# Reordering the end of the recurrent layer, with ScalarE squaring the residual of its last token tile

## The reference

```
x1 = x + (h * silu(gate)) @ w_out            # h: RG-LRU scan
kv = rmsnorm(x1, norm_kv) @ w_kv ;  k, v = split(kv)
k  = rmsnorm_per_head(k, k_norm)
u  = rmsnorm(x1, norm_b) @ w_in_b            # queries and gates of layer B
```

## Time and profile before

| what | us |
|---|---|
| median of 3 runs (1495.4, 1495.9, 1502.24) | 1495.9 |
| the profiled execution | 1499.04 |
| its span, first to last instruction | 1497.3 |
| PE busy | 1459.7 (97%) |
| DVE / ACT / POOL busy | 1035.9 / 700.1 / 259.3 |
| mean granted TensorE clock | 0.994 |

### The profile page before, as it was taken

The page is one execution under the profiler, slowest core; times in us unless marked ns, Lnnn a source line. Parts: engine busy times, 40 slices in busy tenths (PEclk is TensorE's granted clock), DMA queues, the critical chain, the costliest instruction groups (busy, mean ns, idle before and its releaser), DMA issues.

```text
span 1497.3 us, 31229 instructions
## 1 busy us (share of the span) xinstructions
PE 1459.7 (97%) x10634; PEld 1400.7 (94%) x10634; DVE 1035.9 (69%) x2235; ACT 700.1 (47%) x1577; POOL 259.3 (17%) x203
## 2 busy tenths in 40 slices
PE   7999999999999999999899999999998999999999
PEld 7999999999999999998899999999986788888888
DVE  6987857665688888887884534435277877777771
ACT  5433423427787777773362423414145544444440
POOL 0011111001334434443170000000011111111110
PEclk9999999999999999999999999999999999999999
DMA  6565655659855545555523222122345444443312
GB/s 239 168 206 215 214 179 196 219 191 328 301 185 154 170 150 169 169 169 166 176 90 105 76 75 92 51 99 69 94 140 178 122 131 131 124 110 103 106 51 78
DMA packets 215218, 224.20 MB, mean 150 GB/s; under 512 B 61488, under 2 KB 201776, under 8 KB 215088
## 3 DMA queue, kind: packets, MB, share of 16 engines
q1 hardware_dynamic: 202960, 213.19, 45.6%
q10 hardware_dynamic: 12128, 9.39, 1.9%
HBM read 136.33 MB, written 86.44 MB: 149 GB/s over the span
## 4 chain that ended last, share of the span: by engine, by line
PE 63%; DVE 5%; ACT 2%; DMA 1%; issue 1%; SPq 0%; POOL 0%; DVEq 0%; ACTq 0%
PE s_banks L790 22%; PE bank L1812 11%; PE bank L1464 11%; PE s_banks L1431 5%; PE s_banks L1762 3%; PE bank L1447 3%; PE bank L1794 2%; PE bank L1777 2%; PE bank L790 2%; PE bank L1798 2%; ACT m_p L1988 1%; DVE m_nmax L1865 1%; PE bank L1780 1%; DMA x_dram<-r_x 1%; DMA r_x<-xT_dram 1%
## 5 line engine op out<-in xcount | busy, mean ns | idle before, releaser
L1988 ACT ACTIVATE m_p<-s_banks,m_nm 128x192 f32<-128x192 f32 (+2 forms) x264 | 106.1, 414 | 193.0 <-DVE m_nm L1869 193.0
L1812 PE MATMUL bank<-m_y_hi,w_hi_a 128*128 128x256 f32 (+1 forms) x512 | 148.9, 291 | 2.8 <-DVE w_lo_a L910 1.9
L1812 PE MATMUL bank<-m_y_lo,w_hi_a 128*128 128x256 f32 (+1 forms) x512 | 143.8, 281 | 0.0
L1812 PE MATMUL bank<-m_y_hi,w_lo_a 128*128 128x256 f32 (+1 forms) x512 | 143.7, 281 | 0.0
L790 PE MATMUL bank<-a_hi,w_hi_a 128*128 128x352 f32 x384 | 123.6, 322 | 1.3 <-DVE a_out L690 1.1
L790 PE MATMUL bank<-a_hi,w_lo_a 128*128 128x352 f32 x384 | 123.9, 323 | 0.0
L790 PE MATMUL bank<-a_lo,w_hi_a 128*128 128x352 f32 x384 | 123.9, 323 | 0.0
L790 PE MATMUL s_banks<-b_hi,w_hi_b 128*128 128x352 f32 x336 | 111.2, 331 | 0.0
L1464 PE MATMUL bank<-r_y_hi,w_hi_a 128*128 128x264 f32 x384 | 109.3, 285 | 0.6 <-ACT r_std L1359 0.6
L1464 PE MATMUL bank<-r_y_lo,w_hi_a 128*128 128x264 f32 x384 | 109.1, 284 | 0.0
L1464 PE MATMUL bank<-r_y_hi,w_lo_a 128*128 128x264 f32 x384 | 108.8, 283 | 0.0
(11 more groups left out here) (216 smaller groups left out, 4605.3 us busy)
## 6 DMA issues: line engine op xcount, KB each, us to landing
w_raw_b<-weights_dram SPq DMA_DIRECT2D x26, 512.0 KB, 4.3
w_raw_a<-weights_dram SPq DMA_DIRECT2D x25, 512.0 KB, 4.4
sga_dram<-a_out SPq DMA_DIRECT2D x48, 176.0 KB, 3.0
r_xc_hi<-xc_hi_dram SPq DMA_DIRECT2D x32, 264.0 KB, 3.0
r_xc_lo<-xc_lo_dram SPq DMA_DIRECT2D x32, 264.0 KB, 3.1
r_xc<-xc_dram SPq DMA_DIRECT2D x32, 264.0 KB, 3.8
r_sg<-sga_dram SPq DMA_DIRECT2D x32, 264.0 KB, 3.5
r_x<-xT_dram SPq DMA_DIRECT2D x64, 132.0 KB, 2.1
```

Source lines behind the costliest of these rows:

```text
L1812: mm = nc.tensor.matmul(out_bank(ts, blk)[:, 0:width], w[pw][:, kt * P:(kt + 1) * P], (m.y_hi, m.y_lo)[px][tp][:, kt, 0:width], start=(n = ...
L1988: nc.scalar.activation(m.p[:, q, k, v0:192], s_banks[:, 2 * q + e, bp * 192 + v0:(bp + 1) * 192], ACT.Exp, bias=m.nm[:, q, k:k + 1], accum ...
```

## The change

Seven edits. (1) SP: of the four unit loads of turn (8,0), two are issued after the first block's store and the next x load, two after the second's (`gates_free`). (2) The token sum of tile 6 goes to bank 2 and its key sum to bank 3, which the gates no longer use; `out` of the last tile's blocks 1 and 3 then does not wait for the roots. (3) The last tile's key sum goes to bank 7 and runs after layer B's third block, not its first. (4) VectorE squares the last k after B's first block and normalises it after B's fourth (`key_square`, `key_norm`); ScalarE takes the root after B's third (`key_root`). (5) SP loads units 14 and 15 inside B's first pass, at its slots 4 and 5. (6) SP stores the last k and v at slot 6, not 4. (7) The squares of the last tile's residual (eight blocks) are made by ScalarE, in the turn of the block, ahead of that turn's high parts.

```
+        def last_tile(t):
+            return isinstance(t, int) and t == RN - 1
+        def last_sums(t):
+            return isinstance(t, int) and t == RN - 2
+        def key_bank(t):
+            return 5 if not isinstance(t, int) or t < RN - 2 else 3 if t == RN - 2 else 7
...
+            def gates_free(s, g, first):
+                if isinstance(s, int) and (s, g) == (RN, 0):
+                    for k in (first, first + 1):
+                        load_unit(eng, U_B1 + k, r.gates_done, 4 * NG * RN)
...
-                    if isinstance(s, int) and (s, g) == (RN, 0):
-                        for k in range(1, 1 + UNITS_GATE):
-                            load_unit(eng, U_B1 + k, r.gates_done, 4 * NG * RN)
                     if pair:
                         store_x1(pair, 0)
                         load_next(pair, 0)
...
                     if behind:
                         load_x(behind, 0)
+                    gates_free(s, g, 1)
                     if pair:
                         store_x1(pair, 1)
                         load_next(pair, 1)
                     if behind:
                         load_x(behind, 1)
+                    gates_free(s, g, 3)
...
-            for u in range(U_OUT_B - 2, U_OUT_B):
-                load_unit(eng, u, r.kv_mm, NB * RN)
...
+                if not last_tile(t):
+                    need(eng, r.sq_added, mth - 1)
+                    nc.vector.tensor_tensor(r.sq[:, q, :], r.x1[:, q, :], r.x1[:, q, :], ALU.mult).then_inc(r.sq_done, 1)
...
-                if known(s, 2, RN + 1) and g == 3:
-                    tail_norm(s - 2)
+                if known(s, 2, RN) and g == 3:
+                    key_norm(eng, s - 2)
...
                 if known(s, 0, RN - 1):
                     gates(s, g)
+                pair = back_pair(s, g)
+                for q in range(2) if pair and last_tile(pair[0]) else ():
+                    mth = NB * pair[0] + pair[1] + q
+                    eng.wait_ge(r.resid_done, mth + 1)
+                    need(eng, r.sq_added, mth - 1)
+                    nc.scalar.activation(r.sq[:, q, :], r.x1[:, q, :], ACT.Square).then_inc(r.sq_done, 1)
                 for unit in recurrent_units(s, g):
                     high_part(eng, unit)
...
-            if not last:
+            if last:
+                eng.wait_ge(r.kv_read, 2 * RN)
+            elif last_sums(t):
+                eng.wait_ge(r.gates_read, 4 * NG * RN)
+            else:
                 eng.wait_ge(r.resid_done, NB * (t + 1) + 2)
-            nc.tensor.matmul(bank[5][:, 0:RT], head_ones[:, :], r.k2[:, :], start=True, stop=True)\
+            nc.tensor.matmul(bank[key_bank(t)][:, 0:RT], head_ones[:, :], r.k2[:, :], start=True, stop=True)\
...
-                if blk == 1:
+                if blk == 1 and not last_sums(t - 1):
                     need(eng, r.std_done, t)
-                if blk == 3:
+                if blk == 3 and not last_sums(t - 1):
                     need(eng, r.kstd_done, t)
...
-            project_sync(eng, b1, {(1, 4): lambda: store_memory(eng, RN - 1), (1, 12): store_states, (PN, 0): start,
+            project_sync(eng, b1, {(1, 4): lambda: load_unit(eng, U_OUT_B - 2, r.kv_mm, NB * RN),
+                                   (1, 5): lambda: load_unit(eng, U_OUT_B - 1, r.kv_mm, NB * RN),
+                                   (1, 6): lambda: store_memory(eng, RN - 1), (1, 12): store_states, (PN, 0): start,
...
-                if isinstance(s, int) and (s, j) == (1, 0):
+                if isinstance(s, int) and (s, j) == (1, 2):
                     key_sum(eng, RN - 1, True)
...
+                if isinstance(s, int) and (s, j) == (1, 0):
+                    key_square(eng, RN - 1)
+                if isinstance(s, int) and (s, j) == (1, 3):
+                    key_norm(eng, RN - 1)
...
+                if isinstance(s, int) and (s, j) == (1, 2):
+                    key_root(eng, RN - 1)
```

More of the change, by code:

```diff
@@ L1166, in recurrent_sync, with key_square, key_norm @@
             run_steps(eng, 2, RN - 2, RN + 2, body)
-            for u in range(U_OUT_B - 2, U_OUT_B):
-                load_unit(eng, u, r.kv_mm, NB * RN)
             for i in range(2):
                 eng.wait_ge(r.x1_stored[i], 16 * RN * NB // 2)
+        def key_square(eng, t):
+            eng.wait_ge(r.kv_read, 2 * t + 1)
+            need(eng, r.kms_done, t)
+            nc.vector.tensor_tensor(r.k2[:, :], r.k[:, :], r.k[:, :], ALU.mult).then_inc(r.k2_done, 1)
+        def key_norm(eng, t):
+            eng.wait_ge(r.kstd_done, t + 1)
+            nc.vector.reciprocal(r.std[:, :], r.std[:, :]).then_inc(r.krec_done, 1)
+            eng.wait_ge(r.krec_done, t + 1)
+            nc.vector.scalar_tensor_tensor(out=r.k[:, :], in0=r.k[:, :], scalar=vec[:, KN, 0:1], in1=r.std[:, :],
+                                           op0=ALU.mult, op1=ALU.mult).then_inc(r.k_done, 1)
         def recurrent_vector(eng):
@@ L1228, in residual @@
                   .then_inc(r.x1_high, 1)
-                need(eng, r.sq_added, mth - 1)
-                nc.vector.tensor_tensor(r.sq[:, q, :], r.x1[:, q, :], r.x1[:, q, :], ALU.mult).then_inc(r.sq_done, 1)
+                if not last_tile(t):
+                    need(eng, r.sq_added, mth - 1)
+                    nc.vector.tensor_tensor(r.sq[:, q, :], r.x1[:, q, :], r.x1[:, q, :], ALU.mult).then_inc(r.sq_done, 1)
                 eng.wait_ge(r.x1_high, mth + 1)
@@ L1257, in tail_read @@
                 nc.vector.tensor_tensor(r.v[:, :], bank[7][:, 0:RT], r.rstd[:, :], ALU.mult).then_inc(r.kv_read, 1)
[L1258 to L1267, removed]
+                if not (isinstance(t, int) and t == RN - 1):
+                    key_square(eng, t)
             def turn(s, par, g):
@@ L1313, in recurrent_vector, with key_root @@
             eng.wait_ge(r.x1_free, 1)
+        def key_root(eng, t):
+            eng.wait_ge(r.rstd_done, t + 1)
+            eng.wait_ge(r.kms_done, t + 1)
+            nc.scalar.activation(r.std[:, :], bank[key_bank(t)][:, 0:RT], ACT.Sqrt, scale=1.0 / HEAD,
+                                 bias=eps[:, 0:1]).then_inc(r.kstd_done, 1)
         def recurrent_scalar(eng):
@@ L1353, in turn @@
                     need(eng, r.k_done, t)
-                    nc.scalar.activation(r.std[:, :], bank[5][:, 0:RT], ACT.Sqrt, scale=1.0 / D,
+                    nc.scalar.activation(r.std[:, :], bank[2 if last_sums(t) else 5][:, 0:RT], ACT.Sqrt, scale=1.0 / D,
                                          bias=eps[:, 0:1]).then_inc(r.std_done, 1)
[L1356 to L1360, removed]
+                if known(s, 2, RN) and g == 3:
+                    key_root(eng, t)
                 if known(s, 0, RN - 1):
                     gates(s, g)
+                pair = back_pair(s, g)
[4 more added lines that the diff above has]
+                    nc.scalar.activation(r.sq[:, q, :], r.x1[:, q, :], ACT.Square).then_inc(r.sq_done, 1)
                 for unit in recurrent_units(s, g):
@@ L1470, in token_sum @@
                 eng.wait_ge(r.resid_done, NB * (t + 1))
-                nc.tensor.matmul(bank[5][:, 0:RT], ones[:, :], r.acc[:, :], start=True, stop=True)\
+                if last_sums(t):
+                    eng.wait_ge(r.gates_read, 4 * NG * RN)
+                nc.tensor.matmul(bank[2 if last_sums(t) else 5][:, 0:RT], ones[:, :], r.acc[:, :], start=True, stop=True)\
                   .then_inc(r.ms_done, 1)
```

## The result

The change made the kernel **slower**: 1508.25 us (median of 6 runs, 1506.33 to 1510.24) against 1497.5 us (6 runs), a ratio of 1.0072 with a 95% interval of 1.0058 to 1.0085. The forecast was 1490.8 us, the range ended at 1496.0, and "slower by over 0.5%" had a chance of 0.04.

A forecast was written before the change was run, and what follows sets the result against it. PE, busy 97% of the span, was taken as the bound, with about 13 us to win in the seam. 2.6 + 2.7 - 0.9 + 0.9 - 0.8 - 0.3 + 0.9 = 5.1 us saved gave 1490.8 us, range 1487.5 to 1496.0.

The forecast's parts named there:

- Edits 3 and 4: Layer B's start: PE's 0.9 us for the square of k goes; VectorE's reciprocal without the key norm ahead gives nothing.
- The late key sum: Slower rival, chance 0.06: in layer B GpSimd waits for the later key sum; 2.4 us late takes back all 5.1.
- the 2.42 for a square beside GpSimd: Chain to the late key sum: evacuation and square take 1 us, or 3 with GpSimd in the way (2.42 against 0.43).
- Edit 1: Seam: earlier x of (6,6) gives 2.6 us at `out` of (7,0), 2.7 more by the clock; `kv` lead falls to 4.4.
- The two stores behind two unit loads each: SP's queue, (6,5) and (6,6): the latter's store lands after 1.74 us and 2.0 to 2.9 more.
- the 2.7 us of low clock: `out` of (7,0): the clock stays at 2.4 GHz, so it takes 2.93 us instead of 5.61; 2.7 won.
- Nothing in the seam explains that: Profiled execution 3.1 us above the median: not due to the seam, so the same saving was taken from the median.
- the latest start of tile 6's reciprocal: VectorE, behind `residual` of (7,0): the reciprocal starts between 702.0 and 703.3 us; 702.8 was taken.
- Edit 2: `out` of (7,1) and (7,3) no longer wait for the roots; 0.9 us won at (7,3), wait and slower restart.
- Edit 7: ScalarE's order delays VectorE: a new wait of 0.6 us (0.8 with restart) at `kv` of (7,4), 0.3 more at (7,6).
- no table was loaded at a square: ScalarE's squares: no table loads counted; rival with one load in each of four turns loses 5.1 us, chance 0.02.
- The last wait: `kv` of (7,7): the wait stays at 3.1 us, and the lower clock behind it at 1.7.

The follow-up runs named there:

- e13: e10 with the key norm back behind layer B's fourth block, and the store of k and first turn of old values back too: 1503.09 us, ratio 1.0044.
- e5: Edits 3 to 6 alone on the kernel before, with its banks, load order and VectorE's squares: 1507.73 us, ratio 1.0063.
- e6: Changed kernel with the key norm behind layer B's ninth block, not its fourth; store of k and first old values move along: 1507.29 us, ratio 1.0054.
- e7: Changed kernel with both moves: norm behind layer B's ninth block, GpSimd's wait for the key sum behind its unit 8: 1501.0 us, ratio 1.0018.
- e10: e7 without edit 7, and the square of k back at its old place ahead of VectorE's wait for `x1_free`: 1497.3 us, ratio 1.0008.
- e12: The kernel before, unchanged, measured and profiled once more: 1496.5 us, ratio 1.0001.
- e8: The kernel before with SP issuing the next x load ahead of the next unit load in each recurrent turn: 1500.2 us, ratio 1.0018.
- e1: Edits 1 and 2 alone on the kernel before: 1496.17 us, ratio 0.9997.
- e3: Changed kernel with edits 3 to 6 undone, so edits 1, 2 and 7 remain: 1500.81 us, ratio 1.0030.
- e11: e10 with edit 7 added (ScalarE squares the last tile): 1499.63 us, ratio 1.0023.
- e2: Changed kernel without edit 7 (VectorE squares the last tile's residual again): 1507.63 us, ratio 1.0078.
- e4: Changed kernel with GpSimd waiting for the key sum after its low part of unit 8, not unit 3: 1506.14 us, ratio 1.0056.

## Why the prediction was wrong

**Edits 3 and 4, the step that failed.** "VectorE takes up layer B's reciprocal ... without the key norm ahead of it; PE did not wait for it, so nothing." The norm was not saved but moved, and I looked for who waits for the reciprocal, not for who waits at the new place. There it stands in front of the square sums for the head sum, and the term that I had put at nothing measured 8.3 us of PE's time. The idle time of the trace that I had would not have shown it: behind the norm's new place VectorE idled 0.90 us in one block and 0.96 in each of three (of the 4.3 in the groups above, 0.48 lie ahead of that place), its last square sum ended at 776.84 + 0.51 = 777.35 us and PE reached the head sum at 777.64, so 3.78 + 0.29 = 4.07 us stood free for 2.60. What the sum lacked is that a late VectorE's passes get longer (e13). e5 shows that edits 3 to 6 alone bring the wait; e6, e7, e10 and e13 that it takes the norm or GpSimd's lateness, and that either of them is enough.

**The late key sum.** The rival had the right chain and the wrong end. It let PE wait at B's third block and GpSimd have "one block of 3.9 to be ready". PE did not wait there, since VectorE squared k in time. GpSimd did, 6.00 us (1.14 before), and what I took for slack of GpSimd's was the timing of VectorE's passes. Neither its price (1498.5 at 5 us late) nor its chance covers the 8.3.

**Between VectorE and GpSimd.** A pass of 0.5 us takes up to 2.73 beside GpSimd's low part of about 2.5. I had used the 2.42 for a square beside GpSimd as the price of one collision, and did not ask how many collisions a shifted VectorE meets. The Trainium skill, "SBUF — State Buffer", section "Who interferes with whom", says that a VectorE instruction with two SBUF inputs contends with a GpSimd instruction that reads SBUF, and that the ports the two share are an exclusive lock. The trace agrees: L416, L429 and L644 are stretched by as much as is left of a low part, while L690, one of whose inputs is a bank, takes 0.51 to 0.53 in every row shown. The copy L426, which has one SBUF input, was stretched as well (2.54 for 0.33); that sentence does not speak of it.

**The clock behind the wait.** It made 8.3 us into more. From e12 to the changed kernel the head sum comes 783.81 - 775.10 = 8.7 us later and the attention's first product 1101.49 - 1090.44 = 11.05; the 2.3 between them is the low clock after 783 us (0.60 from 783 to 790, 1.00 in e12). The spans differ by 11.3, the medians of the result by 10.8. So nothing behind that adds to the loss.

**Edit 1, mis-sized twice.** The first store landed as forecast (issued 686.48, the next x load at 688.28). The two stores behind two unit loads each, in the chain after the change:

```profile
689.62 4.69 DMA x_dram<-r_x
695.66 5.42 DMA x_dram<-r_x
```

They took 4.69 and 5.42 us, 3.0 and 3.7 above the 1.74 of the earlier trace rows, where I had taken 2.0 to 2.9 as the most. The x of (7,0) came at 703.28, not 700.4 to 702.2, and `kv` of (7,0) waited 1.80 us, not the 1 or so that the lead implied. And the 2.7 us of low clock were no fixed cost of the kernel (e12, e8). Against e12, e1's lead is 2.0 us at `out` of (7,0) (697.47 and 699.50), 1.2 at `kv` of (7,0), 0.7 at `kv` of (7,7): the seam's waits moved from place to place along the x loads. The medians of e1 and its kernel before differ by the same 0.7, which the interval does not tell from nothing. "Nothing in the seam explains that" the profiled execution was 3.1 above the median was wrong: the low clock at `out` of (7,0) did, for the most part (2.5 us of span between the two profiles). By the prediction's own terms, too, the latest start of tile 6's reciprocal was 702.2 + 1.57 = 703.8, not 703.3; it came at 704.55.

**Edit 2** did what was said: no wait for the roots. **Edit 7**: the new wait at `kv` of (7,4) is 0.7 in e3 and e11 (forecast 0.6, though twice 0.73 and 2.93 is 7.3 and not 7.1, which makes it 0.4) and 1.82 in the changed kernel; no table was loaded at a square. Its whole price, 1.1 in the sum, is 2.3 from e10 to e11, 4.6 from e1 to e3, and not to be measured from e2 to the changed kernel (ratios 1.0078 and 1.0072). Why it differs so much stays open, and so does how much of it is the low clock behind `kv` of (7,0), which the profiles of e3 and e11 show and that of the change does not. Edits 5 and 6 were not tried alone.

**The last wait**, 3 us at `kv` of (7,7), stayed as forecast (3.45), and the clock behind it fell.

**What beats both kernels** was not found: e1 and e10 come out within 0.1% of the kernel before.

## What to carry to other kernels

When work is moved off a place where somebody waits for it, read at the new place who waits next on that engine. Free time there is not yet a price of nothing: here 4.07 us stood free for 2.60, and PE still waited 4.5 us with everything else in time (e13), since lateness itself made the passes longer. So ask which passes of other engines the late one will meet, and try the move by itself. Before a low clock or a long transfer is put into a sum, profile the unchanged kernel a second time: what one execution shows and the other does not is no sure gain.

## What the hardware showed that I had not expected

- VectorE passes of 0.5 us took 2.0 to 2.7 us when they met a GpSimd low part of 2.4 to 2.6, a copy (L426, 0.33 and 2.54) as much as passes with two inputs. A reciprocal beside one (L1194) kept its 1.79 us.
- At one and the same place, before `kv` of (7,0), a wait of 1.9 us was followed by the full clock in e10 and by 0.60 to 0.83 in e3; waits of 1.2 to 1.8 us there were followed by the full clock (e7, e1, e13, e4, e2, the change), those of 2.3 and 2.4 us by a lower one (e6, e11: 0.72 from 707 to 713 us).
- A store of 132 KB took 4.7 to 5.6 us behind two loads of 512 KB (the change, e1 to e4, e6) and 3.8 to 4.0 behind one (e8), against 6.7 to 7.5 behind four (the kernel before twice, e5, e8) and 1.74 with none ahead of it.
